# One-hot slot table, raw rows for the gathers, and stores on ScalarE's queue in a mixture-of-experts encoder layer

## The chip, the cores and the metric

The kernel runs on one core of one Trainium2 chip. The time is device microseconds of that core, the median of several runs. PE is TensorE's matrix multiply, PEld its weight load, DVE VectorE, ACT ScalarE, POOL GpSimd and SP SyncE; a name with a q (SPq, POOLq) is that engine's issue of transfers.

## What is computed

Two sequences of 512 and 256 tokens of width 1024 go through one encoder layer: a token mixer (latent attention and mean pooling, with an output projection) and a hierarchical mixture of experts. The part that the change touches:

```
h = x + token_mixer(rms_norm(x, g_attn_norm))
a = rms_norm(h, g_ffn_norm)
gp = softmax(a @ w_group_router + b_group_router)          # 4 groups, the best one is taken
el = (a @ w_expert_router + b_expert_router) of that group # 8 experts, the best two
gate = g_val * e_val / sum(e_val)
y = h + sum over the two experts: gate * (silu(a @ w_gate[e]) * (a @ w_up[e])) @ w_down[e]
```

There are 32 experts of hidden width 256. All is float32.

## The kernel before

The 768 tokens are six tiles of 128. The kernel has three stages: projection of all six tiles, attention and pooling, and then the output projection, in which for each tile i the residual is added, the second norm and the router are computed, and slots are given out. After it come the experts.

**Output projection and routing.** TensorE computes out_half(i, 0) and out_half(i, 1) (lines 693 to 705), 24 matmuls of 512 columns each, and between them transposes tile i-1 (row_transposes, 707), its router logits (715) and ranks within each expert (723), counts of earlier tokens by a triangular matrix. VectorE adds the residual into h_sb (residual, 1158), multiplies h by the norm factor and the gain into rows (second_norm, 1169), picks the group and the experts (route, 1178), computes the gates (route_weights, 1210) and the places in a table (positions, 1224). ACT takes squares and exponentials (934 to 956). POOL turns the sum of squares into the norm factor and writes each token's number to its place in the DRAM table slot_tokens by indirect stores (fill_slots, 1387). SP stores h into out and the normalized rows, with the 32 gates appended (4,224 bytes each), into token_rows (store_rows, 409).

**Experts.** Experts j and j+16 form pair j, and each has a lane of 64 slots. 16 pairs run one after the other on all engines. For a pair TensorE transposes the gathered rows (gather_transposes, 750), computes gate and up (gate_up, 757), and the product with w_down (down, 777); ACT and VectorE copy and apply Silu and gate. POOL gathers the rows of later pairs (gather_pair, 1426) and adds each result to out by an indirect transfer that accumulates (add_rows, 1431). An expert with more than 64 tokens gets an overflow pass in its pair (again); two pairs have one, pair 0 and pair 6, as 18 passes in the trace for 16 pairs and the router's counts say.

**Weights.** A pair's weights are six parts of 1 MiB (load_pair, 254; parts 0 and 1 gate, 2 and 3 up, 4 and 5 down). SP issues them, at most three at once: part n waits for part n-3 to land. There are three buffers. Pair 0's is free early; pair 1's and 2's lie over the output projection's data and are free when its last residual is added. A later pair j waits in refill (438): its first four parts until pair j-3 and its overflow passes have done their gate and up matmuls, the last two until they have done the product with w_down:

```
                def used(kind):
                    sp.wait_ge(kind(main), j - 2)
                    sp.wait_ge(kind(over), passes)
```

**The hand-over.** SP issues parts 0 to 3 of pair 1, waits for all slot stores, reads the table back into idx_all (426), waits until the first gather has landed (431), and only then issues parts 4 and 5 of pair 1 and all of pair 2. POOL's first gather waits for the index, the stored rows and the counts (1407 to 1410).

**The start.** SP loads x, constants, w_in, w_uq, w_ukv, then small tensors (router weights, token numbers, rope gains), the table's initial content and 128 rows of zeros (353 to 380). POOL computes the norm statistics (x_part, 1347); ACT needs the first for k_raw (870).

## Time and profile before

| | |
|---|---|
| time, median of 3 runs | 645.04 us (644.75 to 645.97) |
| the profiled execution | 643.67 us |
| its span, first to last instruction | 642.0 us |
| mean granted TensorE clock | 0.947 |
| busy: PE, DVE, ACT, POOL | 530.8, 223.6, 147.0, 133.2 us |
| moved by DMA | 148.81 MB |

The profiled execution's time is the span and 1.67 us around it. Busy shares are averages over stages with different limits: in the first two stages TensorE is busy and DMA nearly idle, in the expert stage it is the other way round. A wait is put down to what came last.

### The profile page before, as it was taken

What the parts mean: (1) busy time and instruction counts of PE and PEld (TensorE: products, weight loads), DVE (VectorE), ACT (ScalarE), POOL (GpSimd) and SP (SyncE); (2) the same over time, 40 slices, a digit from 0 to 9 for tenths busy, and PEclk for the clock granted to TensorE, in tenths of its full rate; (3) what the DMA queues carried; (4) which work ended last, traced back from release to release, by engine and by line L of the source; (5) the groups of instructions that cost most, each with busy time, mean ns of one, the idle gap of its engine ahead of it and who ended that gap; (6) DMA issues with size and microseconds to landing.
All of it is one profiled execution on the core that took longest, in us unless ns stands there. A gap on an engine that the chain in (4) does not pass through costs nothing.

```text
span 642.0 us, 8839 instructions
## 1 busy us (share of the span) xinstructions
PE 530.8 (83%) x3092; PEld 373.3 (58%) x3093; DVE 223.6 (35%) x602; ACT 147.0 (23%) x310; POOL 133.2 (21%) x200
## 2 busy tenths in 40 slices
PE   5889999997898989999725877989788897777762
PEld 4768988884444568888624545555445564434430
DVE  4743335225959562566650211121211211111110
ACT  6734343322546221121201101010100100000000
POOL 0122232032244000034323102111201232011110
PEclk9999999999999999999856989799989999889997
DMA  8730100000620039243467999999999999999992
GB/s 333 240 142 35 32 2 1 1 0 1 236 72 27 2 137 387 100 132 133 171 227 253 405 374 388 392 367 379 388 393 390 392 392 379 403 390 392 388 363 34
DMA packets 31163, 148.81 MB, mean 232 GB/s; under 512 B 7139, under 2 KB 7798, under 8 KB 18822
## 3 DMA queue, kind: packets, MB, share of 16 engines
q1 hardware_dynamic: 25376, 128.60, 50.2%
q0 software_dynamic: 5712, 19.72, 11.7%
q8 instruction: 22, 0.36, 0.2%
q14 instruction: 15, 0.12, 0.1%
q10 hardware_dynamic: 38, 0.01, 0.0%
HBM read 132.48 MB, written 17.00 MB: 233 GB/s over the span
## 4 chain that ended last, share of the span: by engine, by line
DMA 45%; PE 25%; issue 10%; DVE 6%; POOL 4%; ACT 1%; POOLq 0%; SPq 0%
DMA expert_w<-in_w_down 25%; DMA expert_w<-in_w_up 19%; PE ps L476 4%; PE ps L477 4%; PE ps L481 4%; PE ps L641 3%; POOL slot_tokens L1390 2%; PE ps L582 2%; DVE p_sb L1130 2%; PE ps L596 2%; PE ps L599 1%; PE ps L628 1%; PE ps L516 1%; DMA g_rows<-token_rows,idx_now 1%; PE ps L667 1%
## 5 line engine op out<-in xcount | busy, mean ns | idle before, releaser
L767 PE MATMUL ps<-expert_w,xT 128*64 128x256 f32 x1152 | 132.2, 386 | 16.4 <-DMA expert_w<-in_w_up 6.8
L767 PEld LDWEIGHTS ps<-expert_w,xT 128*64 128x64 f32 x1152 | 97.7, 140 | 55.5 <-issue 27.8
L783 PE MATMUL ps<-expert_w,hT 128*64 128x512 f32 x288 | 76.8, 681 | 23.7 <-DMA expert_w<-in_w_down 13.2
L1432 POOL DMA_INDIRECT out<-y_sb,idx_now x18 | 28.7, 1593 | 202.6 <-DVE y_sb L1302 201.8
L783 PEld LDWEIGHTS ps<-expert_w,hT 128*64 128x64 f32 x288 | 25.5, 155 | 63.1 <-issue 60.7
L1290 DVE SCALAR_TENSOR_TENSOR hid<-s_act,gate,ps 128x256 f32<-128x256 f32 x18 | 11.9, 660 | 141.5 <-ACT s_act L968 141.5
L476 PE MATMUL ps<-w_in_hi,aT_hi 128*128 128x384 f32 (+2 forms) x120 | 43.7, 368 | 0.0
L1302 DVE COPY y_sb<-ps 128x512 f32<-128x512 f32 x18 | 12.5, 692 | 89.5 <-PE ps L783 89.5
L477 PE MATMUL ps<-w_in_lo,aT_hi 128*128 128x384 f32 (+2 forms) x120 | 40.8, 344 | 0.0
L968 ACT ACTIVATE s_act<-ps 128x256 f32<-128x256 f32 x18 | 6.9, 384 | 133.7 <-PE ps L767 133.7
L973 ACT ACTIVATE y_sb<-ps 128x512 f32<-128x512 f32 x18 | 10.8, 597 | 105.6 <-PE ps L783 105.6
L754 PE MATMUL ps<-consts_sb,g_rows 128*128 128x128 f32 x128 | 18.4, 289 | 15.3 <-DMA g_rows<-token_rows,idx_now 15.3
L754 PEld LDWEIGHTS ps<-consts_sb,g_rows 128*128 128x128 f32 x128 | 14.4, 146 | 21.3 <-DMA g_rows<-token_rows,idx_now 16.3
L1381 POOL TENSOR_TENSOR w_out_lo<-w_out_raw,w_out_hi 128x1024 fp32r<-128x1024 f32 x8 | 19.0, 2378 | 34.1 <-ACT w_out_hi L920 34.1
L481 PE MATMUL ps<-w_in_hi,aT_lo 128*128 128x384 f32 (+2 forms) x120 | 24.3, 344 | 0.0
L477 PEld LDWEIGHTS ps<-w_in_lo,aT_hi 128*128 128x128 f32 x120 | 22.6, 188 | 2.6 <-issue 1.2
L476 PEld LDWEIGHTS ps<-w_in_hi,aT_hi 128*128 128x128 f32 x120 | 22.6, 188 | 2.6 <-issue 1.2
L582 PE MATMUL ps<-w_ukv_sb,cT_kv 128*128 128x512 f32 x48 | 21.6, 592 | 0.0
L481 PEld LDWEIGHTS ps<-w_in_hi,aT_lo 128*128 128x128 f32 x120 | 20.6, 188 | 1.6
L1390 POOL DMA_INDIRECT slot_tokens<-tok_ids,idx_pos x12 | 18.7, 1556 | 10.9 <-DVE m_sum L1246 8.3
L596 PE MATMUL ps<-kT,qT 128*128 128x512 f32 (+1 forms) x48 | 20.2, 545 | 0.8 <-DVE rT L1106 0.8
L1413 POOL DMA_INDIRECT g_rows<-token_rows,idx_now x17 | 17.1, 1004 | 14.4 <-POOL idx_now L1424 13.5
(205 smaller groups left out, 856.5 us busy)
## 6 DMA issues: line engine op xcount, KB each, us to landing
expert_w<-in_w_gate SPq DMA_DIRECT2D x32, 1024.0 KB, 9.7
expert_w<-in_w_up SPq DMA_DIRECT2D x32, 1024.0 KB, 8.5
expert_w<-in_w_down SPq DMA_DIRECT2D x32, 1024.0 KB, 10.4
w_in_raw<-in_w_in SPq DMA_DIRECT2D x8, 608.0 KB, 10.3
w_out_raw<-in_w_out SPq DMA_DIRECT2D x8, 512.0 KB, 3.6
token_rows<-rows SPq DMA_DIRECT2D x6, 528.0 KB, 3.4
out<-h_sb SPq DMA_DIRECT2D x6, 512.0 KB, 2.9
x_sb<-in_x_prompt SPq DMA_DIRECT2D x4, 512.0 KB, 9.9
```

What stands on the lines that cost most here:

```text
L476: pe.matmul(dst, l_hi(k), r_hi(k), start=(first and k == ks[0]), stop=False)
L477: pe.matmul(dst, l_hi(k), r_lo(k), start=False, stop=False)
L481: mm = pe.matmul(dst, l_lo(k), r_hi(k), start=False, stop=(last and k == ks[-1]))
L582: mm = pe.matmul(ps[:, 5 + n, :], cT_kv[:, k, :], w_ukv[:, k, n * 512:(n + 1) * 512], start=(k == 0), stop=(k == KKV - 1))
L596: pe.matmul(ps[:, bank + u, 0:n], qT[:, h, q], kT[:, h, keys], start=True, stop=False)
L641: mm = pe.matmul(ps[:, 6 + u, 0:SEQS[s]], v_sb[:, FIRST[s] + c, h * DV:(h + 1) * DV], pT[:, u, c, 0:SEQS[s]], start=(c == 0), stop=(c == T ...
L754: mm = pe.transpose(ps[:, banks + k // 4, (k % 4) * P:(k % 4 + 1) * P], src[:, k * P:(k + 1) * P], ident)
L767: mm = pe.matmul(ps[r, 2, g * FH:(g + 1) * FH], xT[:, q.o, k, r], w_gu(b, lane, k, g), start=(k == 0), stop=(k == KD - 1))
L783: mm = pe.matmul(ps[r, 4 + half, :], hT[:, q.o, k, r], w_dn(b, lane, k, half), start=(k == 0), stop=(k == 1))
L1381: pool.tensor_tensor(w_out_lo[:, k, :], w_out_raw[k % 3][:, :], w_out_hi[:, k, :].bitcast(F32), ALU.subtract).then_inc(w_out_lo_done, 1)
L1390: pool.indirect_dma_start(out=slot_table, out_offset=bass.IndirectOffsetOnAxis(ap=idx_pos[:, i, c:c + 1], axis=0), in_=tok_ids[:, i:i + 1] ...
L1432: pool.indirect_dma_start(out=out, out_offset=bass.IndirectOffsetOnAxis(ap=idx, axis=0), in_=y_sb[:, buf, :], in_offset=None, compute_op=A ...
```

## The change

- The table token_rows holds h itself (4,096 bytes a row); a second table holds 32 gates and the norm factor for each token. The gain g_ffn_norm goes into the router weights (once) and into the copies behind the gathers' transposes (per channel); the norm factor is applied to the logits, to Silu's input and to the gate.
- h is transposed and squared by halves, without a normalized row. out_half becomes out_part, four parts per tile.
- Slots: for each tile two one-hot matrices, token to slot (slot_a) and token to expert with token number, gate and norm factor (slot_b), are multiplied and summed up in PSUM by 2 matmuls; the sum gives idx_all and gate_all for the main passes without DRAM. The DRAM table remains for the overflow passes.
- Gathers have a bounds check, so that empty slots are not fetched.
- Row and gate stores are issued by ACT. The small loads and initial stores of the start are issued by POOL, ahead of its statistics. SP loads pairs 1 and 2 in one go after the last h store.

```diff
@ SP, start and hand-over
-            small = [
-                (rope_tab[:, :, :, :].rearrange("p n t r -> p (n t r)"), a["rope"]),
-                (tok_ids[:, :], a["tokens"]),
-                (w_router[:, :, 0:EG], a["w_group_router"][0].rearrange("(p k) n -> p k n", k=KD)),
-                (w_router[:, :, EG:], a["w_expert_router"][0].rearrange("(p k) n -> p k n", k=KD)),
-            ]
+            small = [(rope_tab[:, :, :, :].rearrange("p n t r -> p (n t r)"), a["rope"])]
...
             for i in range(NT):
                 sp.wait_ge(h_done, 2 * (i + 1))
                 sp.dma_start(out[i * P:(i + 1) * P, :], h_sb[:, i % 2, :]).then_inc(h_stored, 16)
                 if i + 1 < NT:
                     sp.dma_start(x_res[:, :], x_dram(i + 1)).then_inc(x_res_in, 16)
-                else:
-                    load_pair(sp, 1, 1, range(3))
-                if i >= 1:
-                    store_rows(i - 1)
-            load_pair(sp, 1, 1, range(3, 4))
-            store_rows(NT - 1)
-            sp.wait_ge(slots_stored, 2 * NT * 16)
+            load_pair(sp, 1, 1)
+            load_pair(sp, 2, 2)
             sp.wait_ge(counts_done, 1)
-            sp.dma_start(idx_all[:, 0:PAIRS], slot_table[0:BLOCK, :].rearrange("(s j) c -> s (j c)", j=PAIRS)).then_inc(idx_in, 16)
...
-            sp.wait_ge(main.gathered[0], 16)
-            load_pair(sp, 1, 1, range(4, 6))
-            load_pair(sp, 2, 2)
@ TensorE
+            def slots(i):
+                pe.wait_ge(slot_a_done, i + 1)
+                pe.wait_ge(slot_b_done, 3 * (i + 1))
+                for c in range(2):
+                    mm = pe.matmul(ps[:, 5, 0:3 * E], slot_a[:, c, :], slot_b[:, c, :, :].rearrange("t n e -> t (n e)"), start=(i == 0 and c == 0),
+                                   stop=(i == NT - 1 and c == 1))
+                mm.then_inc(slot_mm, 1)
             for i in range(NT):
+                out_part(i, 0, False)
+                if i >= 1:
+                    h_transposes(i - 1, 1)
+                out_part(i, 0, True)
+                if i >= 1:
+                    logits(i - 1, 0)
+                    logits(i - 1, 1)
+                if i >= 2:
+                    slots(i - 2)
+                out_part(i, 1, False)
+                h_transposes(i, 0)
+                out_part(i, 1, True)
+                if i >= 1:
+                    ranks(i - 1)
...
+                blocks = src.rearrange("t (p k) -> t k p", k=KD)
@ ScalarE
+            def store_row(i):
+                if i >= 1:
+                    act.wait_ge(rows_stored, 16 * i)
+                act.dma_start(table[i * P:(i + 1) * P, :], h_sb[:, i % 2, :]).then_inc(rows_stored, 16)
...
+                for k in range(4):
+                    ins = act.activation(xT[:, q.o, k, :], ps[:, bank, k * P:(k + 1) * P], ACT.Copy, scale=g_x[:, k:k + 1])
+                ins.then_inc(q.x_act, 1)
...
+                act.activation(s_act[:, q.o, :], ps[:, 2, 0:FH], ACT.Silu, scale=gate[:, g, 1:2]).then_inc(q.silu_done, 1)
@ VectorE
             for i in range(NT):
+                residual(i, 0)
+                if i >= 1:
+                    route(i - 1)
+                    route_weights(i - 1)
+                residual(i, 1)
+                if i >= 1:
+                    slot_of(i - 1)
+                    table_place(i - 1)
+                    gate_row(i - 1)
             route(NT - 1)
+            route_weights(NT - 1)
+            slot_of(NT - 1)
+            table_place(NT - 1)
+            dve.wait_ge(slot_mm, NT)
+            for lane in range(2):
+                r = slice(lane * LANE, (lane + 1) * LANE)
+                dve.tensor_scalar(idx_all[r, 0:PAIRS], ps[r, 5, PAIRS * lane:PAIRS * (lane + 1)], spare_row[r], None,
+                                  ALU.add).then_inc(idx_done, 1)
...
@ GpSimd
+                for dst, src in ((tok_ids[:, :], a["tokens"]),
+                                 (w_router[:, :, 0:EG], a["w_group_router"][0].rearrange("(k p) n -> p k n", k=KD)),
+                                 (w_router[:, :, EG:], a["w_expert_router"][0].rearrange("(k p) n -> p k n", k=KD)),
+                                 (g_router[:, :], a["g_ffn_norm"][0].rearrange("(k p) -> p k", k=KD)),
+                                 (g_x[:, :], a["g_ffn_norm"][0].rearrange("(p k) -> p k", k=KD))):
+                    pool.dma_start(dst, src).then_inc(router_in, 16)
+            pool.dma_start(slot_table.rearrange("(a b) c -> a (b c)", a=P),
+                           a["slots"].rearrange("(a b) c -> a (b c)", a=P)).then_inc(setup_dram, 16)
+            pool.dma_start(out[T:T + P, :], a["zeros"]).then_inc(setup_dram, 16)
+            step(pool.memset(neg_half[:, :], -0.5))
...
+            def gather(dst, src, idx, done):
+                pool.indirect_dma_start(out=dst, out_offset=None, in_=src, in_offset=bass.IndirectOffsetOnAxis(ap=idx, axis=0),
+                                        bounds_check=T - 1, oob_is_err=False).then_inc(done, 16)
...
+            gather(g_rows[:, 0, :], table, idx_all[:, 0:1], main.gathered[0])
+            gather(g_rows[:, 1, :], table, idx_all[:, 1:2], main.gathered[1])
+            pool.wait_ge(h_stored, 16 * NT)
+            fill_slots(NT - 1)
+            pool.wait_ge(slots_stored, 2 * NT * 16)
+            pool.dma_start(idx_more[:, :], slot_table[BLOCK:2 * BLOCK, :].rearrange("(s j) c -> s (j c)", j=PAIRS)).then_inc(idx_rest_in, 16)
+            pool.wait_ge(counts_done, 1)
+            pool.wait_ge(gates_stored, 16 * NT)
+            pool.wait_ge(idx_rest_in, 16)
             first_more_gather(0)
```

## Rows read from the trace of the kernel before

**Rows 1.** The page's part 4, the chain that ended last, by engine and by line.

```profile
DMA 45%; PE 25%; issue 10%; DVE 6%; POOL 4%; ACT 1%; POOLq 0%; SPq 0%
DMA expert_w<-in_w_down 25%; DMA expert_w<-in_w_up 19%; PE ps L476 4%; PE ps L477 4%; PE ps L481 4%; PE ps L641 3%; POOL slot_tokens L1390 2%; PE ps L582 2%; DVE p_sb L1130 2%; PE ps L596 2%; PE ps L599 1%; PE ps L628 1%; PE ps L516 1%; DMA g_rows<-token_rows,idx_now 1%; PE ps L667 1%
```

**Rows 2.** Windows: from:to, length, busy of each engine (instructions), granted clock, DMA share, GB/s.

```profile
core 0: us, PE busy (x) PEld busy (x) DVE busy (x) ACT busy (x) POOL busy (x), PEclk, DMA share, GB/s
302.00:316.00 14.00, 13.25 (x73) 11.07 (x71) 8.57 (x38) 2.83 (x7) 4.74 (x5) 1.00 0.33 121
316.00:330.00 14.00, 6.07 (x28) 5.32 (x28) 10.79 (x59) 2.27 (x8) 5.75 (x5) 0.56 1.00 342
330.00:345.00 15.00, 2.17 (x9) 1.67 (x9) 2.85 (x17) 0.30 (x1) 6.27 (x10) 0.50 0.40 124
...
400.00:460.00 60.00, 52.98 (x374) 32.96 (x376) 11.58 (x29) 6.92 (x13) 13.13 (x18) 0.94 1.02 379
...
580.00:624.00 44.00, 32.55 (x220) 18.94 (x216) 5.71 (x13) 3.54 (x7) 6.01 (x8) 0.92 1.02 388
```

**Rows 3.** Timeline, TensorE in the expert stage: start, length, line, operation, tiles, count.

```profile
360.12 1.09 PE L754 MATMUL ps<-consts_sb,more_rows 128*128 128x128 f32 x8
...
362.61 7.13 PE L767 MATMUL ps<-expert_w,xT 128*64 128x256 f32 x64 [1.40 <-DVE xT L1278]
...
410.19 7.09 PE L767 MATMUL ps<-expert_w,xT 128*64 128x256 f32 x64
...
423.34 7.11 PE L767 MATMUL ps<-expert_w,xT 128*64 128x256 f32 x64
```

**Rows 4.** Timeline, SP's queue in the same stage, each the issue of transfers.

```profile
342.67 0.80 SPq L266 DMA_DIRECT2D expert_w<-in_w_down  x2
...
370.09 0.89 SPq L266 DMA_DIRECT2D expert_w<-in_w_gate  x2
```

**Rows 5.** Timeline at the end of the kernel, TensorE.

```profile
626.31 3.65 PE L783 MATMUL ps<-expert_w,hT 128*64 128x512 f32 x16 [2.06 <-DMA expert_w<-in_w_down]
```

**Rows 6.** Timeline from the last residual to the first gather's transposes.

```profile
313.43 0.69 DVE L1166 TENSOR_TENSOR h_sb<-ps,x_res 128x512 f32<-128x512 f32 x1 [4.27 <-PE ps L481]
...
325.12 0.16 DVE L1187 TENSOR_TENSOR route_f<-ps,r_bias 128x4 f32<-128x4 f32 x1 [1.12 <-PE ps L720]
...
327.94 0.19 DVE L1208 TENSOR_TENSOR m_sum<-route_f 128x32 bf16<-128x32 f32 x1
...
332.09 0.96 POOL L1390 DMA_INDIRECT slot_tokens<-tok_ids,idx_pos  x1 [0.30 <-issue]
...
338.32 1.01 POOL L1413 DMA_INDIRECT g_rows<-token_rows,idx_now  x1 [0.86 <-DMA idx_all<-in_slots]
...
342.69 1.97 PE L754 MATMUL ps<-consts_sb,g_rows 128*128 128x128 f32 x8 [11.87 <-DMA g_rows<-token_rows,idx_now]
```

**Rows 7.** DMA view: queues with packets, MB, share of span; gathers, median us to landing.

```profile
q1 hardware_dynamic: 25376, 128.60, 50.2%
q0 software_dynamic: 5712, 19.72, 11.7%
...
g_rows<-token_rows,idx_now POOLq DMA_INDIRECT x17, 11.2
```

**Rows 8.** Tile view of slot_tokens, its last line: the landing times of its transfers.

```profile
DMA to landing us min/median/max: 1.7/5.0/8.7
```

**Rows 9.** Timeline of the start: POOL, ACT, VectorE and TensorE.

```profile
6.26 0.57 POOL L1345 TENSOR_TENSOR stats<-stats,neg_half 128x1 f32<-128x1 f32 x1
...
26.91 0.32 ACT L870 ACTIVATE k_raw<-ps,stats 128x64 f32<-128x64 f32 x1
...
36.83 1.43 DVE L1065 TENSOR_TENSOR rope_tab<-rope_tab,q_x 128x256 f32<-128x256 f32 x4 [5.09 <-DMA q_x<-in_g_k_head]
...
41.83 0.66 PE L516 MATMUL ps<-consts_sb,q_n 128*128 128x128 f32 x4 [1.57 <-DVE q_n L1084]
...
47.13 0.63 PE L516 MATMUL ps<-consts_sb,k_n 128*128 128x128 f32 x4 [1.13 <-DVE k_n L1097]
```

More of the change, by code:

```diff
@@ new lines, in store_gates, with slot_part @@
+            def store_gates(i):
+                act.wait_ge(gates_done, i + 1)
+                if i >= 1:
+                    act.wait_ge(gates_stored, 16 * i)
+                act.dma_start(gate_table[i * P:(i + 1) * P, :], gate_rows[:, i % 2, :]).then_inc(gates_stored, 16)
+            def slot_part(i, n, col):
+                for c in range(2):
+                    ins = act.activation(slot_b[:, c, n, :], route_f[:, 224 + E * c:224 + E * (c + 1)], ACT.Copy,
+                                         scale=route_f[:, col(c):col(c) + 1])
+                ins.then_inc(slot_b_done, 1)
@@ L949, in _ @@
                     route_exps(i - 1)
-                act.wait_ge(a2_tr, i + 1)
+                hT_out(i, 0)
                 if i >= 1:
-                    act.wait_ge(lg_mm, i)
-                for half in range(2):
-                    act.activation(a2T[:, 4 * half:4 * half + 4, :], ps[:, 4 + half, :].rearrange("p (k t) -> p k t", k=4),
-                                   ACT.Copy).then_inc(a2T_done, 1)
-            route_exps(NT - 1)
+                    slot_gates(i - 1)
+                square_h(i, 1)
@@ L1324, in pair @@
                 more_passes(j, again)
[L1326 to L1327 removed]
+            gates(0, 0)
             x_copy(main, 0)
@@ L1442, in more_gather @@
                 pool.reg_add(loaded, loaded, 1)
-                gather(more_rows[:, :], idx_now[:, 6:7], over.gathered[0])
+                more_gathers()
             def first_more_gather(j):
@@ L1453, in first_more_gather @@
                     pool.reg_add(firsts, firsts, 1)
-                    gather(more_rows[:, :], idx_now[:, 6:7], over.gathered[0])
+                    more_gathers()
             def more_add(j, n):
```

389 lines of the change are left out of this document (213 added, 176 removed).

## The prediction

> **What bounds the kernel now.** I read in this order: the page's chain, the windows, and the timelines of TensorE and SP's queue in the expert stage, then of the hand-over to it.
>
> The chain that ended last is to 44% the landing of expert weights, w_down 25% and w_up 19% [rows 1]. The windows say the same of the expert stage: from 400 to 460 us and again from 580 to 624 us the sixteen DMA engines are busy all the time (share 1.02) and move 379 and 388 GB/s, while TensorE is busy 32.55 us of the last 44 [rows 2]. So in that stretch every byte costs time and TensorE's work costs none. TensorE alone would go faster: pairs that find their weights loaded follow each other in 13.15 us (410.19 to 423.34) [rows 3], the stream brings a pair in 19.7 us (13 pairs, parts issued from 370.09, the last landed at 626.3, 256.2 us) [rows 4, 5].
>
> Two facts set when the stream may run. In the stretch 330 to 345 us the DMA share is only 0.40 against 1.00 before it [rows 2], because the last parts of pair 1 and all of pair 2 are held back on SP until the first gather has landed (issued at 342.67, [rows 4]). But there are three weight buffers, so pair 3's first part may only be issued when pair 0 no longer needs its buffer, and pair 0 has an overflow pass. SP issues it at 370.09 [rows 4]; that pass's gate and up matmuls run 362.61 to 369.74 [rows 3]. So the filled idle stretch is worth nothing by itself: **the release of pair 0's buffer is what sets the end**, and behind it 13 pairs of traffic.
>
> **The change part by part.**
>
> *Weights of pairs 1 and 2 no longer wait for a gather.* They are 12 parts of 1.05 MB; at 388 GB/s some 32 us from about 316, so they are in SBUF by 350 us. Worth 0 by itself, as said: the buffers are then full, and the stream stands until the release. It costs something: the first gathers and the slot stores now travel beside it.
>
> *From the last residual to the first gather.* Before: last half of h at 313.43, routing of the last tile 325.12 to 328.13, last slot store 332.09, back through DRAM, gather issued at 338.32, landed 342.69 [rows 6]. That is 24.9 us to the issue. After: no normalized row is made, h is transposed by halves, and the slots come out of two matmuls. What is left is VectorE's own queue. Behind the residual (0.7) stand slot_of, table_place and gate_row of tile 4 (19 instructions), then route (17 records before in 3.0 us, 0.18 each [rows 6], and two more), weights 4, slot_of 9, table_place 7, index copies 3: 61 at about 0.2 us is 12.2, with the residual 12.9 us. The last tile's projection ends later: slots(i) adds two f32 matmuls of 96 columns to each of four tiles. One of 256 columns costs 0.22 (32 in 7.09 us [rows 3]); the two cost between 0 and 0.44, I take 0.4, near the nearest row, so 1.6 in four tiles: 315.0. Gather issued at 327.9, 10.4 us earlier.
>
> *Landing of that gather.* Idle, 4.3 us (338.32 to 342.69). In the loaded stage the median is 11.2 [rows 7], with scatter-adds ahead in the queue. Here the weights run beside it but no scatter-add: I take 7.8, both ends kept. Landed 335.7, 7.0 us earlier.
>
> *From there to the release.* Before, 27.05 us (342.69 to 369.74) [rows 3, 6]. ACT now makes four scaled copies for one, twice; 0 to 0.6 us each time beside VectorE's copy, I take 0.4, so 27.9: 363.6. The overflow rows must be there too, wanted 17.4 us after the first landing (360.12 before [rows 3]), now 353.5. Their way is longer than before: two gathers on POOL (329.9), two slot stores (332.2), landing 7 (between the median of 5.0 and the slowest, 8.7 [rows 8]), an index load from POOL 1 plus 5, two more gathers 3, landing 7: about 354. So 364, **6.1 us earlier** than 370.1. Bounds: first gather at its idle 4.3, 2.9 more; every landing at 11.2, see the rival.
>
> *Less gather traffic behind the release.* Fourteen gathers of g_rows and one of overflow rows follow it, 128 rows of 4,224 bytes each: 8.1 MB. With the bounds check empty slots are left out. Running the reference's router gives 1,196 filled slots in pairs 3 to 15, none in the seventeenth gather (a dummy), 2 in the overflow: 4.9 MB. Saved 3.2 MB. The weights' queue takes 322 us for 128.60 MB, 2.5 us per MB; the software queue 75 us for 19.72, 3.8 [rows 7]. So 8.0 to 12.2 if all DMA engines are relieved alike. Filled slots are the low ones of each lane, so engines that serve these may be relieved by little; then only the dummy, the overflow and the 128-byte tails go, 1.3 MB, 3.3 us. I take **6 us**, between 3.3 and 8.0.
>
> *The start.* Gain: VectorE waits 5.09 us for the last small gain load behind the router loads on SP's queue, and TensorE then idles 1.57 and 1.13 us [rows 9]; at most 2.7. Cost: seven loads and stores are now written out by POOL before its first statistics, which k_raw needs at 26.91 [rows 9]. An indirect store of 128 words holds POOL 0.96 us [rows 6]. Three of the seven have 1,024 pieces: between 0.96 each (7 us in all, no harm) and eight times that (27 us in all, from 0.9; with the memset and three statistics steps of about 1.2 us, the power step alone 0.57, they are done at 29.0, 2.1 late). The row is of another kind, so I keep both ends and take gain against cost: **0**, bounds 2.7 faster and 2.1 slower; the 0.6 MB of zeros and slots beside w_in is within these.
>
> The Trainium skill (DMA: Bandwidth & Descriptors, Rules for kernel authors) says that a non-contiguous last dimension lowers to one descriptor per element, and the same page of the Trainium skill (Anatomy of one DMA) says that many descriptors can be emitted before the incremental cost shows. By the first alone the new load of 4-byte gains stands at the dear end, and the sum would be up to 2.1 us higher; by the second it would be 2.7 us lower. No row here shows a direct load from POOL.
>
> *Parts with one answer.* Row and gate stores move to ACT's queue (12 issues of 0.3 to 0.4 us): ACT is busy 2.83 of 14 us in the projection stage [rows 2]: 0. SP loses waits on gates_done and the 512 KB broadcast of g_ffn: 0, it had slack. The transposes read with a stride of eight, and VectorE's copy is a multiply: TensorE has 19.7 minus 13.15, 6.5 us of cover per pair; gone only if eight transposes of 1.09 us [rows 3] took seven times as long. Tail after the last weights: down, copy, scatter-add, unchanged from 626.31 [rows 5].
>
> **Sum.** 6.1 + 6 + 0 = 12.1 us. The profiled execution took 643.67 us (span 642.0); it becomes 631.6. The median of the runs is 1.4 higher: 645.04 becomes 633.
>
> **The rivals.**
> 1. *The overflow rows come late.* For: their way has four landings in a row under a full weight stream. Against: their gather moves a single real row. With 8.7 for the slots and the index load and 11.2 for the gather they land at 365 instead of 354; release 375, 5 us later than before; the 6 us of traffic and 1 us more that the stream then finds nothing in flight give it back: 643.
> 2. *The bounds check saves no transfers,* empty slots cost like full ones. For: no row shows such a gather. Only rows shorter by 128 bytes: 0.5 us in place of 6, so 638.5.
> 3. *The start pays in full and all engines are relieved:* 2.7 and 2 to 3 us more, first gather early: 626.
> 4. *Slower: POOL's queue at the start.* If a piece costs POOL twice what row 332.09 gives, the three loads take 46 us, the statistics come at 52, 25 late, TensorE stands with them: 633 + 25 is about 658, less the 2.7 not won otherwise. It decides from a delay of some 12 us, 1.5 times the row's price per piece. Against: a good part of the 0.96 must be fixed.
>
> **How the numbers follow.** Forecast 0.50, rival 1 0.13, rival 2 0.17, rival 3 0.13, rival 4 0.07. The range leaves out rival 4 and the far ends: 625 to 643. 0.2% (1.3 us) is about what a measurement tells from no change. Faster: all but rival 4 and a third of rival 1, 0.88; same 0.05; slower 0.07.
>
> **What would show it.** SP's queue: pair 3's first gate part at about 364, with 10 us or more before it in which DMA is nearly idle (windows 350 to 364). First g_rows gather issued near 328, landed near 336. Stride of the gate parts behind 400 us 18.5 to 19.3 us. TensorE's idle before L516 gone, k_raw of tile 0 not after 29. Wrong if the release comes before 358 or after 370, if POOL's first statistics come after 30, or if TensorE, not DMA, is busy throughout the expert stage.

## The result, and the profile after

The changed kernel takes 651.36 us (median of 6 runs, 648.72 to 652.37) against 645.50 for the kernel before beside it: the ratio is 1.0074, interval 1.0045 to 1.0103. It is slower, by 0.7%. Measured again with the experiments it takes 650.55 us (12 runs) and the ratio is 1.0049, interval 1.0017 to 1.0080; two of these 12 were slow runs, and a ratio leaves slow runs out. The two ratios together, weighted by their intervals, give 1.0062 (1.0041 to 1.0083), 4 us. I had forecast 633, faster, in a range of 625 to 643.

Single executions differ by some us (the kernel before 642.3 to 650.6), so both kernels were profiled twice. The spans are 642.0 and 644.5 us before, 649.3 and 648.5 after. The first row of the table is the mean of two profiles for each kernel, the stretches below likewise; they add up to the whole.

| stretch | before | after | difference | forecast |
|---|---|---|---|---|
| span | 643.25 | 648.9 | +5.65 | -12.1 |
| start to the load of the first residual (SP) | 231.4 | 235.05 | +3.65 | 0 |
| from there to the first h store | 14.9 | 15.3 | +0.4 | 0 |
| first h store to the last (output projection) | 66.6 | 72.55 | +5.9 | +1.6 |
| last h store to the release of pair 0's buffer | 56.5 | 55.3 | -1.2 | -7.7 |
| behind the release | 273.85 | 270.7 | -3.1 | -6 |

**SP's queue** of the changed kernel (timeline: start, length, line, operation, tiles, count) gives the ends of these stretches; the release is the issue at 379.25, where [rows 4] has 370.09:

```profile
235.05 0.33 SPq L400 DMA_DIRECT2D x_res<-in_x_prompt  x1
...
250.38 0.34 SPq L410 DMA_DIRECT2D out<-h_sb  x1
...
266.25 0.34 SPq L410 DMA_DIRECT2D out<-h_sb  x1
...
322.97 0.34 SPq L410 DMA_DIRECT2D out<-h_sb  x1
...
355.22 2.82 SPq L274 DMA_DIRECT2D expert_w<-in_w_down  x2
379.25 0.88 SPq L274 DMA_DIRECT2D expert_w<-in_w_gate  x2
```

**The chain** of the changed kernel, by engine. Against [rows 1] PE is up by 15 points, issue (time without a wait that the profile shows) down by 8 and POOL down by 3. Such shares say where the chain runs, not what a stage costs; the table does that.

```profile
DMA 48%; PE 40%; DVE 5%; issue 2%; ACT 1%; POOL 1%; SPq 1%; POOLq 0%; ACTq 0%
```

**The start.** Windows (from:to, length, busy of each engine with its instructions, clock, DMA share, GB/s), of the kernel before and then of the changed one. The text ahead of the prediction calls DMA nearly idle in the first two stages. That holds from 40 us on (share 0.08 from 40 to 100 us, 0.22 from 160 to 232), but not here: in the second 10 us the share of the kernel before is 1.02. It moved 280 GB/s in the first 10 us and only 218 in the third 10. In the changed kernel the third is still nearly full, and TensorE, with less work ready in the second, shows a granted clock of 0.83 in the fourth. The clock alone tells little: the second profile of the kernel before has 0.84 there, that of the changed kernel 0.66.

```profile
0.00:10.00 10.00, 2.25 (x9) 1.75 (x10) 1.88 (x7) 4.95 (x7) 1.31 (x9) 1.00 0.77 280
10.00:20.00 10.00, 9.91 (x45) 9.18 (x46) 9.85 (x7) 8.79 (x7) 0.00 (x0) 1.00 1.02 417
20.00:30.00 10.00, 7.55 (x46) 6.66 (x45) 6.54 (x9) 8.04 (x19) 2.71 (x7) 1.00 0.70 218
30.00:40.00 10.00, 10.00 (x48) 8.03 (x46) 4.13 (x8) 1.00 (x2) 0.57 (x2) 1.00 0.47 176
```
```profile
0.00:10.00 10.00, 2.26 (x9) 1.76 (x10) 1.89 (x7) 3.65 (x6) 6.45 (x16) 1.00 0.78 222
10.00:20.00 10.00, 7.45 (x31) 6.83 (x32) 6.01 (x5) 6.62 (x6) 0.00 (x0) 1.00 1.00 400
20.00:30.00 10.00, 8.59 (x51) 7.71 (x49) 7.58 (x6) 7.80 (x9) 1.20 (x3) 1.00 0.95 368
30.00:40.00 10.00, 7.58 (x28) 6.29 (x29) 6.78 (x13) 5.68 (x16) 1.54 (x4) 0.83 0.30 107
```

POOL's issues and the first row of w_in (timelines of POOL and ScalarE):

```profile
1.46 0.74 POOL L1442 DMA_DIRECT2D tok_ids<-in_tokens  x1 [0.87 <-POOLq L1626]
2.20 1.00 POOL L1442 DMA_DIRECT2D w_router<-in_w_group_router  x1
3.16 0.93 POOL L1442 DMA_DIRECT2D w_router<-in_w_expert_router  x1
...
6.02 0.54 POOL L1445 DMA_DIRECT2D out<-in_zeros  x1
6.52 0.16 POOL L1446 MEMSET neg_half<- 128x8 f32 x1
6.79 0.19 POOL L1455 TENSOR_SCALAR stats<-stats 128x1 f32<-128x1 f32 x1
```
```profile
11.10 1.31 ACT L855 ACTIVATE w_in_hi<-w_in_raw,gains 128x1216 fp32r<-128x1216 f32 x1 [3.40 <-DMA w_in_raw<-in_w_in]
...
30.76 0.32 ACT L877 ACTIVATE k_raw<-ps,stats 128x64 f32<-128x64 f32 x1
```

POOL is done at 6.5 us; it was never late. But ScalarE waits 3.40 us for the first row of w_in (in the second profile 1.12 for the first and 1.65 for the next), and k_raw comes at 30.76 and 29.97 instead of 26.91 [rows 9] and 26.50.

**Hand-over and overflow pass**, timelines of TensorE and POOL. The rows wanted by L761 at 344.51 were issued at 334.90. The overflow rows land behind a round trip that has a wait of 10.29 us in it, TensorE waits 3.40 for them, and their gate and up matmuls take 9.95 us instead of 7.13 [rows 3] (in the second profile 10.48, 1.14 and 8.78):

```profile
344.51 1.97 PE L761 MATMUL ps<-consts_sb,g_rows 128*128 128x128 f32 x8 [11.21 <-DMA g_rows<-token_rows,idx_all]
...
365.73 1.97 PE L761 MATMUL ps<-consts_sb,more_rows 128*128 128x128 f32 x8 [3.40 <-DMA more_gate<-token_gates,idx_now]
368.94 9.95 PE L774 MATMUL ps<-expert_w,xT 128*64 128x256 f32 x64 [1.23 <-ACT xT L1020]
```
```profile
334.90 1.07 POOL L1514 DMA_INDIRECT g_rows<-token_rows,idx_all  x1 [5.03 <-DVE gate_all L1346]
...
338.91 0.98 POOL L1495 DMA_INDIRECT slot_tokens<-tok_ids,idx_pos  x1 [0.30 <-issue]
350.18 0.60 POOL L1606 DMA_DIRECT2D idx_more<-slot_tokens  x1 [10.29 <-DMA slot_tokens<-tok_ids,idx_pos]
...
357.66 1.07 POOL L1514 DMA_INDIRECT more_rows<-token_rows,idx_now  x1 [1.00 <-POOL idx_now L1555]
```

**Queues** (packets, MB, share of 16 engines), against [rows 7]: ACT's queue q10 now carries the row and gate stores, and POOL's queue q0 moves 3.2 MB less. That this is also the 3.2 MB forecast behind the release is chance: q0 has taken over 0.76 MB of the start, so that all its gathers together have lost about 4 MB, and those behind the release are a part of them.

```profile
q1 hardware_dynamic: 21504, 123.53, 48.5%
q0 software_dynamic: 6048, 16.53, 10.6%
q10 hardware_dynamic: 1766, 3.26, 1.7%
```

### The profile page after: what moved, and what is told of

The parts are those of the page before. It is cut to its first block, busy times and chain, and to the rows that moved or that the text cites. A ratio compares the mean times of both kernels' runs of the same rounds, so it can differ in the third digit from the quotient of the medians.

```text
span 649.3 us, 9073 instructions
## 1 busy us (share of the span) xinstructions
PE 536.2 (83%) x3116; PEld 377.7 (58%) x3117; DVE 217.8 (34%) x642; ACT 168.7 (26%) x412; POOL 136.2 (21%) x208
## 4 chain that ended last, share of the span: by engine, by line
DMA 48%; PE 40%; DVE 5%; issue 2%; ACT 1%; POOL 1%; SPq 1%; POOLq 0%; ACTq 0%
DMA expert_w<-in_w_down 21%; DMA expert_w<-in_w_up 18%; PE ps L458 8%; PE ps L459 7%; PE ps L463 7%; DMA w_uq_raw<-in_w_uq 3%; PE ps L623 3%; PE ps L564 3%; PE ps L578 2%; DMA slot_tokens<-tok_ids,idx_pos 2%; DMA x_res<-in_x_prompt 2%; PE ps L774 2%; DVE p_sb L1192 1%; PE ps L581 1%; PE ps L610 1%
## 5 line engine op out<-in xcount | busy, mean ns | idle before, releaser
L774 PE MATMUL ps<-expert_w,xT 128*64 128x256 f32 x1152 | 136.6, 395 | 20.1 <-DMA expert_w<-in_w_up 7.5
L790 PE MATMUL ps<-expert_w,hT 128*64 128x512 f32 x288 | 71.9, 644 | 19.1 <-DMA expert_w<-in_w_down 10.5
L1026 ACT ACTIVATE s_act<-ps,gate 128x256 f32<-128x256 f32 x18 | 8.5, 473 | 140.6 <-PE ps L774 140.6
L761 PE MATMUL ps<-consts_sb,g_rows 128*128 128x128 f32 x128 | 19.3, 297 | 15.0 <-DMA g_rows<-token_rows,idx_all 11.2
L1020 ACT ACTIVATE xT<-ps,g_x 128x128 f32<-128x128 f32 x72 | 20.5, 368 | 35.5 <-PE ps L761 35.5
L761 PEld LDWEIGHTS ps<-consts_sb,g_rows 128*128 128x128 f32 x128 | 16.1, 196 | 21.0 <-DMA g_rows<-token_rows,idx_all 11.3
L1501 POOL TENSOR_SCALAR route_f<-route_f 128x1 f32<-128x1 f32 x6 | 2.0, 338 | 99.9 <-ACT h_junk L954 99.9
L1229 DVE TENSOR_TENSOR h_sb<-ps,x_res 128x512 f32<-128x512 f32 x12 | 8.3, 691 | 40.5 <-PE ps L463 17.4
```

Source lines behind the costliest of these rows:

```text
L761: mm = pe.transpose(ps[:, banks + k // 4, (k % 4) * P:(k % 4 + 1) * P], blocks[:, k, :], ident)
L774: mm = pe.matmul(ps[r, 2, g * FH:(g + 1) * FH], xT[:, q.o, k, r], w_gu(b, lane, k, g), start=(k == 0), stop=(k == KD - 1))
L790: mm = pe.matmul(ps[r, 4 + half, :], hT[:, q.o, k, r], w_dn(b, lane, k, half), start=(k == 0), stop=(k == 1))
L1020: ins = act.activation(xT[:, q.o, k, :], ps[:, bank, k * P:(k + 1) * P], ACT.Copy, scale=g_x[:, k:k + 1])
```

## The experiments

All edits are against the changed kernel unless said otherwise, "spans" are those of the profiled execution. The changed kernel and the kernel before were themselves run as marks. The experiments ran on four chips, each time with the kernel before beside them (medians 645.7 to 646.6). So a gain or loss against the changed kernel is told from the two ratios to the kernel before, with 1.0062 for the changed kernel; one thousandth is 0.65 us, and the number behind ± is the 95% interval of the difference.

> The changed kernel itself, as the mark for the experiments on this chip, where the kernel before has spread from 642 to 649 us. If the experiments so far are worth what their traces say, it takes about 650 us (ratio to before 1.005 to 1.009); if their gains were the chip's own (rival), about 646.

Measured 650.55 us, ratio 1.0049 (1.0017 to 1.0080), span 648.5. The theory holds, at the lower end of its ratios.

> The kernel before itself, for a second profiled execution on this chip. If one execution stands for the others (theory): first residual's load at 232 to 233.5, release of pair 0's buffer at 369.5 to 371.5, 271 to 273 us behind it. Rival: the stretches vary by 2 us or more from execution to execution, and differences of that size between single traces say nothing.

Measured span 644.5: first residual's load at 230.19, release at 368.71, 275.8 us behind it. The rival holds for two of three: the start differs by 2.4 us and the stretch behind the release by 3.9 between two executions of one kernel. So a difference between single traces below some 3 us isn't used alone; what follows goes by medians, or by places that several traces show.

### The start

```diff
-                    pool.dma_start(dst, src).then_inc(router_in, 16)
-            pool.dma_start(slot_table.rearrange("(a b) c -> a (b c)", a=P),
-                           a["slots"].rearrange("(a b) c -> a (b c)", a=P)).then_inc(setup_dram, 16)
-            pool.dma_start(out[T:T + P, :], a["zeros"]).then_inc(setup_dram, 16)
             step(pool.memset(neg_half[:, :], -0.5))
...
                 pool.tensor_scalar(S[:, 44:48], S[:, 40:44], S[:, 25:26], None, ALU.mult).then_inc(k_rstd, 1)
+                if i == 0:
...
+                            pool.dma_start(dst, src).then_inc(router_in, 16)
+                    pool.dma_start(slot_table.rearrange("(a b) c -> a (b c)", a=P),
+                                   a["slots"].rearrange("(a b) c -> a (b c)", a=P)).then_inc(setup_dram, 16)
+                    pool.dma_start(out[T:T + P, :], a["zeros"]).then_inc(setup_dram, 16)
@ VectorE
-                if i == 1:
+                if i == 2:
                     dve.wait_ge(router_in, 16 * N_ROUTER)
```

> Edit: the seven transfers that POOL issues first (token numbers, router weights and gains in small pieces, empty slot table, zeros) go behind POOL's statistics of tile 0, as they stood in the kernel before. Theory A (traffic: they run beside the loads of w_in and w_uq, so that tile 0's weights come late): k_raw of tile 0 back from 30.8 to 27 us or earlier, the first residual's load issued at about 230 (232.6 before, 235.1 in the changed kernel), the run 2.5 to 5 us shorter than the changed kernel's 651.4, so 646.5 to 649. Rival B (the later start comes from SP's order of loads, which this doesn't touch): k_raw stays at 30 to 31 and the time within 1 us of 651.4.

Measured 645.23 us, ratio 0.9976 (0.9953 to 0.9998): 5.6 us (±2.0) under the changed kernel. k_raw at 27.39, first residual's load at 228.93. Its windows are close to those of the kernel before again, and the granted clock stays at 1.00:

```profile
0.00:10.00 10.00, 2.26 (x9) 1.76 (x10) 1.88 (x7) 4.89 (x7) 1.32 (x9) 1.00 0.78 272
10.00:20.00 10.00, 9.79 (x38) 9.03 (x39) 9.72 (x7) 8.71 (x8) 0.00 (x0) 1.00 1.02 415
20.00:30.00 10.00, 8.43 (x50) 7.44 (x49) 6.17 (x8) 7.80 (x18) 2.29 (x7) 1.00 0.66 235
30.00:40.00 10.00, 10.00 (x47) 8.09 (x47) 6.79 (x15) 3.81 (x7) 2.66 (x7) 1.00 0.26 97
```

Theory A holds; VectorE's moved multiply has no part in it, as it runs at 57.15 us in the changed kernel, long after the loads, and waits for nothing. The gain that I had counted at the start is real too: in the five kernels with all seven late (this one and the four combined ones below) the load comes at 226.7 to 228.9, in the kernel before at 230.2 and 232.6. Two more runs part the seven transfers. With only the slot table and the zeros moved late:

> Edit: of the seven transfers that POOL issues first, only the two of large pieces (empty slot table and zeros) go behind tile 0's statistics; the small-piece loads (router weights, gains, token numbers) stay at the start. Theory A1 (bytes: the 0.6 MB of the two takes DMA from w_in): k_raw of tile 0 at 27 to 28 us as with all seven late (27.4), the first residual's load at 229 to 231. Rival A2 (the small pieces of the router loads cost the time): k_raw stays at 29.5 to 31, the first residual's load at 233 to 235 and no gain in the time.

Measured 650.12 us, ratio 1.0030 (0.9994 to 1.0067), 2.1 us (±2.7) under the changed kernel; k_raw 28.3, residual's load 232.47. With only the five small-piece loads moved late, and VectorE's wait with them:

> Edit: of POOL's seven first transfers only the five small-piece loads (router weights, gains, token numbers) go behind tile 0's statistics, the slot table and the zeros stay at the start. With all seven late the first residual's load came at 228.9, with the two large ones late alone at 232.5, with none at 235.0. Theory (each part of the traffic beside w_in costs, the small pieces more than their 0.15 MB): 231 to 232, k_raw of tile 0 at 28.5 to 29.5, the time 2 to 4 us under the changed kernel's. Rival (only the bytes count, so 0.15 of 0.76 MB): 234 and no gain.

Measured 645.74 us, ratio 0.9994 (0.9969 to 1.0018), 4.4 us (±2.1) under the changed kernel; k_raw 28.4, residual's load 233.15. Neither run meets either of its expectations whole. The two ratios differ by 2.3 us (±2.8), so the times don't part the two groups; by the single traces each costs about 2 us. What the traces do show is that the small-piece loads cost more than their 0.15 of the 0.76 MB. With them at the start the first 10 us move 221 to 230 GB/s (eight traces), without them 272 to 304 (eight traces), at a DMA share of 0.75 to 0.81 in all. And the packets of the small-piece loads occupied the DMA engines for 20 us in sum (run e1b_setup_late), those of the slot table and the zeros, four times the bytes, for 31 us (run e1c_router_late): 1.2 and 2.0 us for each of the sixteen. Together that is less than the 5.6 us of the whole effect; what the rest is stays open.

### Weights beside the rows

```diff
-            load_pair(sp, 1, 1)
+            load_pair(sp, 1, 1, range(4))
+            sp.wait_ge(main.gathered[0], 16)
+            load_pair(sp, 1, 1, range(4, 6))
             load_pair(sp, 2, 2)
```

> Edit: SP again issues the last two of pair 1's parts and all of pair 2 only when the rows of pair 0 are gathered, as in the kernel before; all else as changed. Theory A (the weights that now run without a hold slow the rows, the slot stores and the overflow rows of pair 0): landing of the first gather 7 to 8 us instead of 9.6, the overflow rows at about 361 instead of 365.7, the release of pair 0's buffer at about 374 instead of 379.3, the run 4 to 6 us shorter than 651.4: 645.5 to 647.5. Rival B (what is held comes later and nothing is gained, since DMA then has the same bytes to move): release earlier, but pair 2's parts late, time within 1.5 us of 651.4. Rival C (the chain of waits of POOL sets the overflow rows, 0.6 to 1 us of issue and some 5 us of idle latency each): release earlier by under 2 us.

Measured 645.40 us, ratio 0.9989 (0.9963 to 1.0015): 4.7 us (±2.2) under the changed kernel; release at 372.5, 50.5 us behind the last h store instead of 55.3. Overflow pass on TensorE:

```profile
362.62 1.16 PE L763 MATMUL ps<-consts_sb,more_rows 128*128 128x128 f32 x8 [1.47 <-DMA more_gate<-token_gates,idx_now]
365.01 7.13 PE L776 MATMUL ps<-expert_w,xT 128*64 128x256 f32 x64 [1.24 <-ACT xT L1022]
```

Theory A holds in time and place, but half of its mechanism was wrong: the first rows still land 9.2 us behind their issue. What moved is the slot stores (POOL waits 7.65 us for them, not 10.3), so the overflow rows come 3 us earlier (2 us, counted from the last h store), and the pass runs at 7.13 us instead of 8.78 and 9.95.

### The second residual

```diff
-            sp.dma_start(x_res[:, :], x_dram(0)).then_inc(x_res_in, 16)
+            for i in range(2):
+                sp.dma_start(x_res[:, i, :], x_dram(i)).then_inc(x_res_in[i], 16)
```

> Edit: the residual's tile gets a second buffer and the first two tiles are loaded ahead of pair 0's weights; one semaphore for each buffer. Theory A (the 16 us between the first two tiles of the output projection are the wait for the second residual behind pair 0's weights): that interval falls from 15.95 to under 13 us, the last row store from 323 to about 320, the time 2 to 3 us shorter than 651.4: 648.5 to 649.5. Rival B (the weights of pair 0 shift by the same and the overflow rows or PE take it back): stage shorter, time within 1 us of 651.4.

Measured 647.67 us, ratio 1.0010 (0.9984 to 1.0037): 3.4 us (±2.2) under the changed kernel. The first interval is 13.2 us instead of 15.8 to 15.9, the stage 70.2. The wait that it removes stands in VectorE's timeline of the changed kernel:

```profile
261.01 0.69 DVE L1229 TENSOR_TENSOR h_sb<-ps,x_res 128x512 f32<-128x512 f32 x1 [10.66 <-DMA x_res<-in_x_prompt]
...
265.53 0.69 DVE L1229 TENSOR_TENSOR h_sb<-ps,x_res 128x512 f32<-128x512 f32 x1
```

In the kernel before this residual was as late: it was loaded at 247.89 and used at 257.32, where the changed kernel has 250.77 and 261.01. But there the second half followed at 258.57. The changed kernel's VectorE has the routing of tile 0 between the two halves, so that all of it runs behind the late load, and the second half comes at 265.53 only.

### The skipped slots

```diff
-    table = nc.dram_tensor("token_rows", [T, D], F32, kind="Internal").ap()
+    table = nc.dram_tensor("token_rows", [T + P, D], F32, kind="Internal").ap()
...
-                                        bounds_check=T - 1, oob_is_err=False).then_inc(done, 16)
+                                        bounds_check=rows - 1, oob_is_err=False).then_inc(done, 16)
```

> Edit: the table of raw rows has 128 rows more, zeros, and the bound of the gathers lies behind them, so that an empty slot fetches a row of zeros as in the kernel before; the gate's gather still skips. Theory A (skipped rows are worth their bytes, 3.2 MB): queue 0 moves 19.7 MB, first rows land 2 us later, behind the release 275 to 276 us instead of 270, the time 5 to 7 us longer than the changed kernel's. Rival B (skipping is worth little because the weights' stream was not held up by the gathers): under 2 us longer.

Measured 654.71 us, ratio 1.0143 (1.0112 to 1.0175): 5.2 us (±2.4) over the changed kernel, queue 0 moves 20.72 MB, 4.19 more, of which 0.52 are the store of the zeros. So skipping saves about 5 us, as theory A has it (the added store is in it; the first residual's load, at 235.26, shows no cost of it). By the single traces 2 us of it lie ahead of the release and 2 behind, where theory A had 5. The page's packet line, of the changed kernel and then of this one:

```profile
DMA packets 29357, 143.82 MB, mean 221 GB/s; under 512 B 6419, under 2 KB 7110, under 8 KB 17014
```
```profile
DMA packets 29389, 148.02 MB, mean 227 GB/s; under 512 B 5539, under 2 KB 6230, under 8 KB 17030
```

The number of packets is the same but for 32, while 880 more of them are under 512 bytes when slots are skipped. A skipped row is not a packet less, it is a small packet in place of one of 4 KB (3.67 MB are 896 rows; 16 of the 32 packets that the store of the zeros adds are small as well). These small packets cost next to nothing: from 400 to 620 us queue 0 has 1058 packets of 4 bytes in the changed kernel and 464 in this one, and they took 9 ns each, those of 4,096 bytes 263 and 244 ns. The rows of the gathers were then also dealt out differently (the first lines of the edit; the constants for the spare row and the experts' numbers follow it):

```diff
+    p = np.arange(LANE)
+    place = ((p & 3) + 4 * (p >> 5)) * 8 + ((p >> 2) & 7)
-    c[:, C_IOTA:C_IOTA + P] = np.arange(P)
+    c[:, C_IOTA:C_IOTA + P] = np.concatenate([place, LANE + place])
```

> Edit: slot numbers are dealt to partitions in another order, so that an expert's filled slots no longer sit on the first partitions of its lane but are spread over all 16 DMA queues' engines; same rows gathered and skipped. Theory A (the 3.2 MB that the skipped slots save come off a few engines alone, the fullest engine has as much as before, so only 1.9 of the forecast 6 us came behind the release): from the release of pair 0's buffer to the end 266 to 268 us instead of 270.1, the time 2 to 4 us shorter than 651.4. Rival B (gather traffic is cheap per byte beside the weights, or the engines are level already): 270 and within 1 us of 651.4.

Measured 646.90 us, ratio 1.0009 (0.9981 to 1.0037): 3.4 us (±2.3) under the changed kernel, 268.0 us behind the release. The window from 520 to 580 us shows where it comes from. The DMA share is 1.02 in all of these, but the rate isn't the same. In this order: the kernel before, the changed kernel, the one without skipping, the one with the slots spread:

```profile
520.00:580.00 60.00, 46.78 (x317) 27.64 (x318) 9.12 (x21) 5.38 (x11) 10.78 (x14) 0.94 1.02 394
```
```profile
520.00:580.00 60.00, 46.38 (x332) 29.70 (x330) 8.58 (x19) 8.25 (x23) 11.99 (x16) 0.97 1.02 374
```
```profile
520.00:580.00 60.00, 47.25 (x346) 30.41 (x342) 9.28 (x20) 8.87 (x24) 12.27 (x16) 0.97 1.02 388
```
```profile
520.00:580.00 60.00, 48.70 (x314) 28.67 (x314) 8.89 (x20) 8.38 (x23) 10.63 (x13) 0.91 1.02 390
```

A window of 60 us is short: the second profile of the changed kernel has 379 here, and the run with the hold 388. From 400 to 620 us it is clearer. The eight traces of kernels that skip and don't spread have 381 to 385 GB/s; the two of the kernel before, the one without skipping and the one with the slots spread all have 389. From one pair's first gate part to the next, over ten pairs behind 400 us, it takes 19.6 us in the kernel before, 19.3 and 19.4 in the changed one and 18.9 with the spread. So skipping lowers the rate, and dealing the same slots out over the partitions restores it.

Why it does is not shown. Theory A has some engines left with more than the others. The profile doesn't list single engines, but engines that run dry would lower the mean share, and that stays at 1.02. What differs is the time of the weights' packets of 8,192 bytes: 316 to 319 ns on average where slots are skipped and not spread, 312 to 313 in the kernel before, without skipping and in every kernel with the spread.

### The order in the last tile

```diff
-                if i >= 1:
+                if i >= 1 and not last:
                     logits(i - 1, 0)
                     logits(i - 1, 1)
...
                 out_part(i, 1, True)
+                if last:
+                    logits(i - 1, 0)
+                    logits(i - 1, 1)
+                    slots(i - 2)
```

> Edit: in the last of the six tiles of the output projection, tile 4's logits and tile 3's slot matmuls stand behind the projection's last matmuls instead of before them, as in the kernel before. Theory A (they were moved, not added: the last row store comes earlier and what follows it later): last row store 1.8 to 2.1 us earlier (321 instead of 322.9), 1.8 to 2.1 us more from there to the first gather, release and time unchanged within 1 us. Rival B (the work hides behind waits of the last tile's routing): release 1 to 2 us earlier and the time too.

Measured 654.25 us, ratio 1.0122 (1.0090 to 1.0154): 3.9 us (±2.5) over the changed kernel. Both expectations are wrong. VectorE's program has the routing of tile 4 ahead of the last half of the last residual, so the logits of tile 4 delay the last h store itself: it comes at 325.37, 2.5 us later, not 2 us earlier, and 17.7 us behind the store before it instead of 14.3. Logits early in the tile are right, and cost TensorE time before the store.

### Together

The combined kernel has the late start, the hold, the second residual buffer and the spread slots:

> Edit: the four edits tried so far together (POOL's first transfers behind tile 0's statistics, the hold of pair 1's last parts and of pair 2, two buffers for the residual, slot numbers spread over the partitions). If their gains lie behind one another on the path (theory A): first residual load at about 229, last row store at about 314.5, release of pair 0's buffer at 364 to 366, 268 to 270 us behind it, so a span of 633 to 636 and a time of 635 to 638, 1.3 to 1.8% under before. Rival B (all relieve the same bound, the total of bytes): 643 to 645.

Measured 634.86 us, ratio 0.9838 (0.9804 to 0.9872): 1.6% under the kernel before, 14.5 us (±2.6) under the changed kernel, where the four single gains add up to 17.1 (5.6, 4.7, 3.4, 3.4). Within the noise they lie behind one another, as theory A says. The profiled execution was the fastest of the six: residual's load 227.84, last h store 314.0, release 364.1, 265.7 us behind it.

> Edit: the combined kernel without the spreading of the slot numbers. Theory (an expert's filled slots sit on the first partitions of its lane, so that the skipped ones relieve some DMA engines alone): 267.5 to 270 us behind the release instead of 265.7, the time 638 to 640 against 634.9 of the combined kernel. Rival (the spreading did nothing, its 3.6 us alone were the chip's spread): 266 and 634 to 636.

Measured 637.62 us, ratio 0.9879 (0.9847 to 0.9910), 272.0 us behind the release, and from 385 to 605 us 383 GB/s against 389 in the combined kernel. The theory's direction holds; by the ratios the size is 2.6 us (±3.0), so the time alone wouldn't show it, but it agrees with the 3.4 us of the spread by itself. Then the weights beside the rows once more:

```diff
-            load_pair(sp, 1, 1, range(4))
             sp.wait_ge(main.gathered[0], 16)
-            load_pair(sp, 1, 1, range(4, 6))
+            load_pair(sp, 1, 1, range(0, 6))
```

> Edit: the combined kernel, with all six parts of pair 1 held until pair 0's rows are gathered (four of them went ahead in the combined kernel). Theory A (the weights beside the rows make them land late): first gather landed 4.5 to 5.5 us behind its issue instead of 8.5, release of pair 0's buffer 3 us or more earlier than 364.1 (counted from the last row store: 46 to 47 us instead of 50.1). The 12 MB of pairs 1 and 2 then take 31 us at 390 GB/s from about 331, so to about 362, just by the release: time 631 to 633, or, if the stream is late (rival B), release at 361 but behind it 3 us more and the time as before, 634.9. Rival C (the rows wait for their own small pieces): landing still over 7.5 us, no gain or a loss of some us.

> Edit: the combined kernel, with pair 1's parts 2 to 5 held and parts 0 and 1 let through. Theory A: first gather landed 5 to 6.5 us behind its issue, release 2 to 3 us earlier than 364.1, time 631.5 to 633.5. Rival C (own pieces): 8 us and no gain.

Measured 636.81 us (ratio 0.9865, 0.9839 to 0.9890) and 636.34 (0.9859, 0.9833 to 0.9885): no gain over 634.86. Theory A is right on the landing, 4.1 and 4.4 us instead of 8.5, and wrong on what it brings: the release comes 53.4 and 51.8 us behind the last h store instead of 50.1. TensorE, with all of pair 1 held:

```profile
330.78 1.97 PE L767 MATMUL ps<-consts_sb,g_rows 128*128 128x128 f32 x8 [5.73 <-DMA g_rows<-token_rows,idx_all]
...
354.40 1.97 PE L767 MATMUL ps<-consts_sb,more_rows 128*128 128x128 f32 x8 [4.46 <-DMA more_gate<-token_gates,idx_now]
357.60 10.12 PE L780 MATMUL ps<-expert_w,xT 128*64 128x256 f32 x64 [1.23 <-ACT xT L1026]
```

and in the combined kernel:

```profile
334.46 1.97 PE L768 MATMUL ps<-consts_sb,g_rows 128*128 128x128 f32 x8 [10.07 <-DMA g_rows<-token_rows,idx_all]
...
354.27 1.15 PE L768 MATMUL ps<-consts_sb,more_rows 128*128 128x128 f32 x8 [1.43 <-DMA more_gate<-token_gates,idx_now]
356.65 7.13 PE L781 MATMUL ps<-expert_w,xT 128*64 128x256 f32 x64 [1.24 <-ACT xT L1027]
```

The first rows come 3.7 us earlier and the overflow rows at the same time, 354.3 and 354.4. Nearly all the gain becomes TensorE's wait (4.46 us instead of 1.43), and the pass that follows it costs 3 us more. The windows of the two around that pass, the one with pair 1 held first, show a granted clock of 0.56 against 1.00:

```profile
355.00:365.00 10.00, 8.77 (x49) 5.25 (x49) 0.69 (x1) 1.14 (x4) 0.00 (x0) 0.56 1.03 371
```
```profile
355.00:365.00 10.00, 7.54 (x68) 4.73 (x67) 1.15 (x2) 1.62 (x5) 1.16 (x1) 1.00 0.71 236
```

So the overflow rows' way sets the release, not the first rows.

## Why the prediction was wrong, point by point

- **What bounds the kernel** was right: behind the release the DMA share is 1.02, and the late start, the hold and the order in the last tile moved the release by -5.6, -5.7 and +3.8 us from its mean of 378.2 and the time by -5.6, -4.7 and +3.9.
- **The start, taken as 0 (bounds -2.7 and +2.1), was +3.65.** The step that failed was "the 0.6 MB of zeros and slots beside w_in is within these". I priced POOL's instructions and put the traffic itself at nothing, and no row of before had the same transfers run beside w_in: on SP's queue they stood behind it, on POOL's they compete with it. POOL's issues cost 0.54 to 1.00 us each, the cheap end. The traffic, 0.76 MB with the small pieces that the step doesn't name, cost 5.6 us of time (shown by moving it late). The gain beneath it, up to 2.7, was right: TensorE's waits of 1.57 and 1.13 us are gone in the changed kernel.
- **The output projection, taken as +1.6, was +5.9.** The step that failed is "slots(i) adds two f32 matmuls", as if nothing else moved. From the traces: the slot matmuls take 0.66 us a tile by their records and lengthen a tile by 0.5, four tiles 2.1 (forecast 1.6). That term was nearly right; the other two were missing. Logits of the previous tile now stand ahead of the tile's last half and so fall once more between the first and the last store, 1.4 (first interval 13.2 with the second buffer, 11.8 before). The second residual is late behind pair 0's weights and now holds up the routing of tile 0 and the second half with it, 2.6 of the interval (shown by the second buffer). Sum 6.1.
- **From the last h store to the first gather** 11.9 us in the changed kernel (322.97 to 334.90); forecast 12.9 from the residual, so 12.2 from the store. Right: 0.2 us for each of VectorE's 61 instructions was the right price.
- **Landing of the first gather, taken as 7.8 us, was 9.6 and 10.4.** It is 4.1 and 4.4 with all or most of pair 1 held (shown). But this term is worth little, as the two holds show.
- **From the landing to the release, taken as 27.9 us, was 34.7 (344.51 to 379.25) and 31.9 in the second profile.** This is the miss of that stretch. The step "landing 7" for the slot stores was 10.3 of waiting, and TensorE behind its wait ran the pass in 8.8 to 10.1 us instead of 7.13, which no term had. The sum of the overflow rows' way was also added up wrong: 332.2, 7, 1 plus 5, 3 and 7 make 355.2, not 354. Rival 1 described this mechanism and had the rows at 365; I gave it 0.13. That they landed at 365.7 is luck: the start and the output projection had put all of this later by themselves. Counted from the last h store the rows came after 42.8 and 42.7 us, where my sum has 38 to 39 and rival 1 has 49; the release came after 56.3 and 54.3, forecast 48, rival 59. The price of early weights, 4.7 us, is shown by the hold.
- **Gather traffic, taken as 6 us.** The stretch behind the release gained 3.1. The skipping is worth 5.2 us (±2.4) of the time by the run without it, about 2 of them behind the release by single traces. The step that failed is the price for each MB taken from the rate of before: with the slots skipped the rate itself fell from 389 to between 381 and 385 GB/s. I had named a cause in the sum's lower bound, that the filled slots are the low ones of each lane. That the place of the slots matters is shown by the spread; that some engines are left with more is not. Rival 2 (the check saves nothing) is out.
- **The signs.** The release at 379.3 and 377.1 lies outside 358 to 370, k_raw comes after 29, and the first gather is issued at 334.9, not 328; DMA is nearly idle ahead of the release (37 GB/s from 367 to 379 us), as expected.
- **Rival 4** was the one that ended slower, and is out too: it had POOL's queue late, where POOL was done at 6.5 us. The place was right, the mechanism wasn't.
- Where the Trainium skill bears on it: POOL's direct load of 4,096 bytes in 1,024 pieces of 4 bytes took 0.92 us to issue, that of the same bytes in 128 pieces of 32 bytes 0.60, the other two of 1,024 pieces 0.93 and 1.00. The Trainium skill (DMA: Bandwidth & Descriptors, Anatomy of one DMA) says that many descriptors can be emitted before the incremental cost shows. These rows agree, as far as the issuing engine goes: 896 more pieces took 0.3 to 0.4 us more. What the pieces cost the other queues is in no such row.

The five stretches make +5.65 us in the profiles; the two ratios say +3.2 and +4.8. With four small edits the changed kernel gives 634.9. That this is near the 633 forecast is in part luck: the late start and the hold take back two placements of the change, some 10 us, but the second buffer and the spread, some 7 us, are new and stood in no sum.

## What to carry to other kernels

When a transfer is moved to another queue, cost the traffic that it now runs beside, not only the instruction that issues it: a queue is also an order, and giving it up set 0.76 MB that is needed late beside the first weights, which are needed at once. Where a result is needed early and another later, look at which of the two sets the release; an earlier first gather is worth nothing if the overflow rows come no earlier. And the bytes that a transfer leaves out aren't saved at the old rate: look at the GB/s at full share as well, and try other partitions for the left-out rows.

## What the runs showed of the hardware that I had not expected

- Small pieces weigh more than their bytes beside a full stream: with the five loads of 0.15 MB at the start the first 10 us moved 221 to 230 GB/s, without them 272 to 304, at the same DMA share of 0.75 to 0.81. Their packets occupied the DMA engines for 20 us in sum, those of 0.61 MB in large pieces for 31.
- At one and the same DMA share of 1.02 the queues moved 381 to 385 GB/s from 400 to 620 us with the empty slots skipped, and 389 without skipping or with the slots spread, so a full share says nothing of the rate.
- The 64 matmuls of the overflow pass took 7.13 us behind waits of 1.21, 1.43 and 1.47 us, and 8.5 to 10.1 behind all of the longer ones (9.85 behind 2.21, 8.90 behind 3.00, 9.95 behind 3.40, 8.47 behind 4.33, 10.12 behind 4.46), without an order among these; in one execution it was 8.78 behind 1.14. The granted clock of 0.56 over the slowest of them is a mix of 1.2 and 2.4 GHz, and 1.00 over the fastest is 2.4 GHz. A wait on the path was so charged twice.
- A gather with a bounds check still makes a packet for each slot that it skips, of 4 bytes and 9 ns.
- The first indirect gather of pair 0's rows landed after 4.1 to 4.4 us without expert weights beside it and after 8.2 to 10.9 with them.
